# A two-layer diffusion trunk: norm and next modulation joined, half of the norm's subtractions on GpSimd, the output written by channel halves

## The reference, cut to what matters

```python
def modulate(x, shift, scale):
    return x * (1 + scale) + shift

def trunk_layer(x, mod, p, ctx):
    shift, scale, gate = mod[:, :, :, 0], mod[:, :, :, 1], mod[:, :, :, 2]
    h = modulate(x, shift[:, :, 0], scale[:, :, 0])
    x = layer_norm(ALPHA * x + 0.5 * gate[:, :, 0] * swiglu(h, p['ffn_w_gu'][0], p['ffn_w_down'][0]),
                   p['ln_g'][0], p['ln_b'][0])
    h = modulate(x, shift[:, :, 1], scale[:, :, 1])
    u, state = token_mixing(h, p, ctx)
    x = layer_norm(ALPHA * x + gate[:, :, 1] * u, p['ln_g'][1], p['ln_b'][1])
    h = modulate(x, shift[:, :, 2], scale[:, :, 2])
    x = layer_norm(ALPHA * x + 0.5 * gate[:, :, 2] * swiglu(h, p['ffn_w_gu'][1], p['ffn_w_down'][1]),
                   p['ln_g'][2], p['ln_b'][2])
    return x, state
```

## Time and profile before

| | |
|---|---|
| median of 3 runs | 3199.32 us (3198.49 to 3204.26) |
| the profiled execution | 3201.78 us, of which the span of its records is 3200.0 us |
| PE busy | 2974.8 us, 93% of the span |
| DVE, ACT, POOL busy | 1289.7, 914.8 and 144.8 us |
| PE in the chain that ended last | 84% of the span |

### The profile page before, as it was taken

How to read it: one execution, slowest core, us unless ns; L and a number is a source line. 1 busy time by engine, 2 the same in 40 slices (tenths; PEclk the granted TensorE clock), 3 DMA queues, 4 the chain that set the end, 5 groups by cost and what they waited for, 6 DMA issues and landing times.

```text
span 3200.0 us, 46489 instructions
## 1 busy us (share of the span) xinstructions
PE 2974.8 (93%) x20109; PEld 2613.6 (82%) x20109; DVE 1289.7 (40%) x1789; ACT 914.8 (29%) x1270; POOL 144.8 (5%) x88
## 2 busy tenths in 40 slices
PE   6999998998789899999979999989987998999997
PEld 5999997776546599999979999967755455999996
DVE  3233235445545442322542322364363546233226
ACT  3221223322245132222252212233223434221222
POOL 0000000104200000000000000001050000000000
PEclk8999999999889999999989999999997999999998
DMA  8223233103220122322532232421142101223221
GB/s 297 66 66 87 79 107 116 53 27 118 93 86 7 47 66 66 85 78 72 162 105 72 65 91 70 134 72 53 53 143 96 33 1 53 79 59 93 72 62 52
DMA packets 359017, 259.03 MB, mean 81 GB/s; under 512 B 27152, under 2 KB 310100, under 8 KB 358740
## 3 DMA queue, kind: packets, MB, share of 16 engines
q1 hardware_dynamic: 358868, 256.85, 26.6%
HBM read 253.25 MB, written 3.57 MB: 80 GB/s over the span
## 4 chain that ended last, share of the span: by engine, by line
PE 84%; DVE 8%; ACT 3%; DMA 2%; issue 1%; SPq 1%; POOL 0%; DVEq 0%; ACTq 0%; PEldq 0%; POOLq 0%
PE banks L729 54%; PE banks L645 15%; PE banks L596 2%; ACT arena L1250 2%; PE banks L1164 1%; PE banks L844 1%; PE banks L1187 1%; DVE x_res L1808 1%; PE banks L1015 1%; PE banks L1201 1%; DMA w_slots<-in_w_mod 1%; PE banks L1157 1%; DMA w_slots<-in_ffn_w_down 1%; DVE w_split L1687 1%; PE banks L910 1%
## 5 line engine op out<-in xcount | busy, mean ns | idle before, releaser
L729 PE MATMUL banks<-h_hi,w_split 128*128 128x320 f32 x5376 | 1184.5, 309 | 1.1 <-DVE mod L1636 1.1
L729 PEld LDWEIGHTS banks<-h_hi,w_split 128*128 128x128 f32 x5376 | 899.4, 188 | 1.5 <-issue 1.5
L729 PE MATMUL banks<-h_lo,w_split 128*128 128x320 f32 x2688 | 830.6, 309 | 0.0
L729 PE MATMUL banks<-hid_hi,w_split 128*128 128x320 f32 x2816 | 624.5, 310 | 0.1
L1687 DVE TENSOR_TENSOR w_split<-w_slots,w_split 128x2048 fp32r<-128x2048 f32 x152 | 348.3, 2292 | 422.1 <-ACT w_split L1250 422.0
L729 PEld LDWEIGHTS banks<-h_lo,w_split 128*128 128x128 f32 x2688 | 504.5, 188 | 0.0
L1250 ACT ACTIVATE arena<-banks 128x640 f32<-128x640 f32 (+8 forms) x336 | 170.1, 537 | 1137.9 <-PE banks L729 804.4
L729 PEld LDWEIGHTS banks<-hid_hi,w_split 128*128 128x128 f32 x2816 | 472.2, 188 | 2.0 <-issue 1.6
L729 PE MATMUL banks<-hid_lo,w_split 128*128 128x320 f32 x1408 | 435.3, 309 | 0.0
L1250 ACT ACTIVATE w_split<-w_slots 128x2048 fp32r<-128x2048 f32 x152 | 290.1, 1909 | 405.6 <-PE banks L729 371.2
L1751 DVE TENSOR_TENSOR arena<-arena,banks 128x640 f32<-128x640 f32 x88 | 72.2, 821 | 767.1 <-ACT arena L1250 767.1
(11 more groups left out here) (258 smaller groups left out, 2563.0 us busy)
## 6 DMA issues: line engine op xcount, KB each, us to landing
w_slots<-in_ffn_w_gu SPq DMA_DIRECT2D x176, 512.0 KB, 5.1
w_slots<-in_ffn_w_down SPq DMA_DIRECT2D x64, 384.0 KB, 3.7
w_slots<-in_w_mod SPq DMA_DIRECT2D x12, 2048.0 KB, 7.9
arena<-in_w_mod SPq DMA_DIRECT2D x10, 2048.0 KB, 12.9
w_slots<-in_ffn_w_down SPq DMA_DIRECT2D x64, 320.0 KB, 4.3
h_mod<-in_w_mod SPq DMA_DIRECT2D x8, 2048.0 KB, 7.9
mixed<-in_w_mod SPq DMA_DIRECT2D x6, 2048.0 KB, 8.9
w_slots<-in_w_in SPq DMA_DIRECT2D x6, 2048.0 KB, 8.0
```

The lines of the kernel that those rows point to most:

```text
L729: ins = mm(banks[:, b0 + hf, 0:HALF], w[:, k, :], x[:, k, t], start=w is wlo and k == 0, stop=w is whi and x is hi and k == kt - 1, skip_g ...
```

## The change

Gain and bias of a norm are no longer applied to `X` where a modulation follows. VectorE forms, from the modulation's scale and shift and the norm's gain and bias, a joint factor and addend (`compose`, three instructions of 128 x 8 for each half of the channels, into `JOINT`), and ScalarE's `modulate` applies these to the normed tile straight away (`normed` in place of `affine`). The residual gets gain and bias with ALPHA in `scale_residual`, 8 instructions for one, from vectors scaled at the start (`LNS`). Only the last norm of layer 1 still has its own gain and bias on ScalarE.

GpSimd subtracts `DELTA` from tiles 4 to 7 (`shift(sub)` in its list, four instructions a norm), VectorE keeps tiles 0 to 3 and waits for `shifted` ahead of tiles 4 to 7. Modulation pieces 12 and 14 (first halves of shift and scale) change places with 13 and 15: the former are now computed in the token mixers, the latter in norm 1. In `ffn(0)`, `parameters()` stands ahead of `settle(0, 4)`. SyncE fills the third modulation of a swiglu after down job 6's weights, not after job 5's. Low parts of the input tiles are made within norm 2 as in norm 1. At the end transposes, copies and stores go through half 0 of all token tiles first, then half 1, with 10 stores of 256 KB.

Left out of the diff: semaphore names and counts, the allocation of `LNS` and `JOINT`, and places where 12 and 14 are only renamed.

```diff
--- before.py
+++ after.py
...
@@ -147,7 +147,7 @@
-FIRST_MODS, RING_MODS = (0, 2, 1, 3, 4, 5), (10, 11, 13, 15, 16, 17)
+FIRST_MODS, RING_MODS = (0, 2, 1, 3, 4, 5), (10, 11, 12, 14, 16, 17)
@@ -160,7 +160,7 @@
     if sub < 2:
-        return [((l, 8), (l, 9)), ((l, 12), (l, 14))][sub]
+        return [((l, 8), (l, 9)), ((l, 13), (l, 15))][sub]
     return [(l + 1, 2), (l + 1, 3)] if l + 1 < DEPTH else []
...
@@ -268,7 +270,7 @@
                     MOD_AT[x] = (hmod, mixed)[n][:, 0:SLOT]
-            MOD_AT[l, 12], MOD_AT[l, 14] = hmod[:, 0:SLOT], arena[:, 0:SLOT]
+            MOD_AT[l, 13], MOD_AT[l, 15] = hmod[:, 0:SLOT], arena[:, 0:SLOT]
             for i in RING_MODS:
...
@@ -510,7 +512,7 @@
                                     fill_mod(*mods[1])
-                                elif m == 5:
+                                elif m == 6:
                                     sp.wait_ge(mod_row, mod_at[mods[0]] + 1)
...
@@ -571,11 +573,13 @@
-            for t in range(NCH):
-                sp.wait_ge(fin_copy, 2 * t + 2)
-                dst = a["y_s"][0, t * P:(t + 1) * P, :] if t < 4 else a["y_p"][0]
-                sp.dma_start(dst, XIN[:, t, :]).then_inc(fin_store, 16)
-            sp.wait_ge(fin_store, 16 * NCH)
+            for n in range(2 * NCH):
+                half, t = n // NCH, n % NCH
+                cols = slice(half * 512, (half + 1) * 512)
+                sp.wait_ge(fin_copy, n + 1)
+                dst = a["y_s"][0, t * P:(t + 1) * P, cols] if t < 4 else a["y_p"][0, :, cols]
+                sp.dma_start(dst, XIN[:, t, cols]).then_inc(fin_store, 16)
+            sp.wait_ge(fin_store, 32 * NCH)
...
@@ -1219,9 +1223,9 @@
-            pe.wait_ge(s["affine"], DEPTH * 24)
             for n in range(2 * NCH):
-                t, half = n // 2, n % 2
+                half, t = n // NCH, n % NCH
+                pe.wait_ge(s["affine"], 4 * half + 4)
                 if n >= 4:
@@ -1294,21 +1298,24 @@
-                    MOD = MODS[l]
+                    plain = l == 0 and sub == 0
+                    shift, scale = (MODS[l][:, sub, i] if plain else JOINT[:, i] for i in range(2))
                     for m in range(KT_M):
-                        if m % 4 == 0:
-                            act.wait_ge(mod_done, max(mod_at[l, 6 * sub + m // 4], mod_at[l, 6 * sub + 2 + m // 4]) + 1)
+                        if m % 4 == 0 and plain:
+                            act.wait_ge(mod_done, max(mod_at[l, m // 4], mod_at[l, 2 + m // 4]) + 1)
+                        elif m % 4 == 0:
+                            act.wait_ge(s["composed"], o["composed"] + 2 * (sub - 1) + m // 4 + 1)
                         if m == 0 and (l or sub):
-                            act.wait_ge(mod_row, mod_at[l, (3, 9, 14)[sub]] + 1)
+                            act.wait_ge(mod_row, mod_at[l, (3, 9, 15)[sub]] + 1)
                         if l or sub:
-                            act.wait_ge(s["affine"], o["affine"] + 8 * (sub - 1) + m + 1)
+                            act.wait_ge(s["normed"], o["normed"] + 8 * (sub - 1) + m + 1)
                         at = 8 * (sub // 2) + m
...
                             ins = f(dst[:, t0:t0 + n], X[:, m, t0:t0 + n], ACT.Identity,
-                                    scale=MOD[:, sub, 1, m, g:g + 1], bias=MOD[:, sub, 0, m, g:g + 1])
+                                    scale=scale[:, m, g:g + 1], bias=shift[:, m, g:g + 1])
                         ins.then_inc(s["modded"], 1)
@@ -1612,8 +1619,8 @@
                 layer_norm(2, (lambda: weights_hi(2 * FFN_JOBS + 1)) if l + 1 < DEPTH else None)
-                for m in range(KT_M):
-                    act.wait_ge(s["normed"], o["normed"] + m + 1)
+                for m in range(KT_M if l + 1 == DEPTH else 0):
+                    act.wait_ge(s["normed"], o["normed"] + 16 + m + 1)
                     f(X[:, m, :], X[:, m, :], ACT.Identity, scale=PTS1[l][:, R_LNG + 16 + m:R_LNG + 17 + m],
@@ -1647,6 +1654,7 @@
                     link(ins)
+                link(v.tensor_scalar(LNS[l][:], PTS1[l][:, R_LNG:R_LNG + 48], float(ALPHA), None, ALU.mult))
             dve.sem_inc(par1_ready, 1)
@@ -1686,13 +1694,31 @@
-                def input_lo_tile(sub, m):
-                    dve.wait_ge(s["h_hi"], o["h_hi"] + 8 * (sub // 2) + m + 1)
+                def input_lo_tile(n, m):
+
+                    dve.wait_ge(s["h_hi"], o["h_hi"] + 8 * n + m + 1)
                     v.tensor_tensor(HLO[:, m], GATE[:, m % 2], HHI[:, m].bitcast(F32), ALU.subtract).then_inc(s["h_lo"], 1)
...
                     dve.wait_ge(s["modded"], o["modded"] + 8 * (sub + 1))
-                    link(v.tensor_scalar(X, X, float(ALPHA), None, ALU.mult))
+                    if l == 0 and sub == 0:
+                        link(v.tensor_scalar(X, X, float(ALPHA), None, ALU.mult))
+                        return
+                    ln, at = (LNS[l], 8 * (sub - 1)) if sub else (LNS[l - 1], 16)
+                    for m in range(KT_M):
+                        ins = v.tensor_scalar(X[:, m, :], X[:, m, :], ln[:, at + m:at + m + 1], ln[:, 24 + at + m:25 + at + m], ALU.mult, ALU.add)
+                    link(ins)
+
+                def compose(sub, half):
+
+                    ln, sn = (l, sub + 1) if sub < 2 else (l + 1, 0)
+                    ms = slice(4 * half, 4 * half + 4)
+                    shift, scale = MODS[ln][:, sn, 0, ms], MODS[ln][:, sn, 1, ms]
+                    dve.wait_ge(mod_done, max(mod_at[ln, 6 * sn + half], mod_at[ln, 6 * sn + 2 + half]) + 1)
+                    gain, bias = (bc(PTS1[l][:, r + 8 * sub + 4 * half:r + 8 * sub + 4 * half + 4].unsqueeze(2), [P, 4, 2]) for r in (R_LNG, R_LNB))
+                    link(v.tensor_tensor(JOINT[:, 0, ms], scale, bias, ALU.mult))
+                    v.tensor_tensor(JOINT[:, 1, ms], scale, gain, ALU.mult)
+                    finish(v.tensor_tensor(JOINT[:, 0, ms], JOINT[:, 0, ms], shift, ALU.add), "composed", 2 * sub + half + 1)
@@ -1789,12 +1815,12 @@
                                 dve.wait_ge(f_freed[n % 2], o["f_freed"][n % 2] + n // 2 + 1)
+                                if sub == 0 and m == 4:
+                                    parameters()
                                 settle(sub, m)
...
                                     mod_add(*mods[m // 5], 3)
-                                if sub == 0 and m == 4:
-                                    parameters()
@@ -1816,39 +1842,32 @@
                         mod_add(*mods[0], 3)
+                        compose(sub, 0)
                     if meanwhile:
...
                     shift(1)
-                    if not meanwhile:
-                        shift(2)
                     dve.wait_ge(s["rstd"], o["rstd"] + sub + 1)
                     for m in range(KT_M):
-                        if m == 4 and meanwhile:
-                            shift(2)
-                        if m == 6:
-                            shift(3)
                         if m == 1 and mods:
                             mod_add(*mods[1], 3)
-                        if sub == 2:
-                            v.tensor_tensor(X[:, m, :], X[:, m, :], RS[:], ALU.mult).then_inc(s["normed"], 1)
-                            continue
-                        link(v.tensor_tensor(X[:, m, :], X[:, m, :], RS[:], ALU.mult))
-                        v.tensor_scalar(X[:, m, :], X[:, m, :], PTS1[l][:, R_LNG + 8 * sub + m:R_LNG + 8 * sub + m + 1],
-                                        PTS1[l][:, R_LNB + 8 * sub + m:R_LNB + 8 * sub + m + 1], ALU.mult, ALU.add).then_inc(s["affine"], 1)
-                        if sub == 1:
-                            if m >= 2:
-                                input_lo_tile(2, m - 2)
+                            compose(sub, 1)
+                        if m >= 4:
+                            dve.wait_ge(s["shifted"], o["shifted"] + 4 * sub + m - 3)
+                        v.tensor_tensor(X[:, m, :], X[:, m, :], RS[:], ALU.mult).then_inc(s["normed"], 1)
+                        if m >= 2 and sub and mods:
+                            input_lo_tile(sub, m - 2)
                     if sub == 1:
                         weights_lo(FFN_JOBS + 1)
-                        input_lo_tile(2, 6)
-                        input_lo_tile(2, 7)
+                    if sub and mods:
+                        input_lo_tile(sub, 6)
+                        input_lo_tile(sub, 7)
...
                     weights_lo(0)
-                for m in range(KT_M):
-                    input_lo_tile(0, m)
-                    if l == 0 and m == 3:
-                        weights_lo(1)
+                    for m in range(KT_M):
+                        input_lo_tile(0, m)
+                        if m == 3:
+                            weights_lo(1)
                 scale_residual(0)
@@ -2140,6 +2159,12 @@
                 o = offsets[l]
+                def shift(sub):
+                    pool.wait_ge(s["delta_copied"], o["delta_copied"] + sub + 1)
```

(20 more changed lines are left out.)

## The result

The changed kernel takes 3182.06 us (median of 4 runs, 3177.82 to 3186.89), the kernel before on the same chip 3198.90. The ratio is 0.9946, 95% interval 0.9930 to 0.9962: 17 us faster (12 to 22). The forecast was 3179.2 us, in a range of 3161 to 3188.

The account below looks back on a forecast made before the run. TensorE holds 84% of the chain, so only its idle time and the tail can be won. Parameters -17.4, norm 0 +3.8, norm 1 +0.6, norm 2 -5.0, end -2.1: -20.1 us, giving 3179.2 us (range 3161 to 3188).

Parts of the forecast that it names:

- Parameters first: Swiglu 0, both layers: TensorE's 12.9 us wait for `par` goes, with slow matmuls and products behind it; -17.4 us.
- The price of a shift: Norms and end: GpSimd's shifts alternate with VectorE's two-input instructions, one whole instruction at a time, 1.2 us per shift.
- norm 0: Norm before the first projection, twice: ScalarE's first modulation starts later, +1.9 us each; -0.65 each without contention.
- The end: Last norm to the final stores: copies end earlier despite two GpSimd shifts among the multiplications, -2.1 us; -4.1 without contention.
- No contention: Rival, chance 0.20: GpSimd's shifts do not hold VectorE up; -37.1 us in sum, 3162.2 us.
- norm 1: Norm before the second swiglu, twice: last low parts and k-tiles end later, +0.3 us each; -3.0 each without contention.
- norm 2: Norm from layer 0 into layer 1: first modulation takes the first affine's place, -5.0 us; -8.3 without contention.
- GpSimd as a wait of its own: Rival, chance 0.06: each GpSimd shift is 2.5 us of work in norms and end; +28.6 us, 3207.8 us.
- `par` as a wait that moves: Rival, chance 0.06: TensorE's wait in swiglu 0 only moves to job 7's bank or weights; 17.4 us back, 3196.6 us.

Follow-up runs that it names:

- e2_vector: The changed kernel with the shifts of tiles 4 to 7 back on VectorE at their former places; 3163.31 us, ratio 0.9886 to the kernel before.
- e3_late: The changed kernel, but GpSimd waits for the first multiplication by rstd before its shifts, in all norms but the last; 3176.47 us, ratio 0.9925 to before.
- e4_half: The changed kernel with each GpSimd shift cut into two instructions of 320 columns; 3179.66 us, ratio 0.9934 to the kernel before.
- e5_own: e2_vector plus GpSimd copies, two-input subtractions or fills on data no other engine touches, one kind in each of three norms; 3168.55 us, one run.

## Why the prediction was right

*Parameters first*: -17.03 measured, -17.4 forecast. The wait went and nothing took its place, with or without SyncE's fill moved. The one step that was off is the product behind the matmuls: I took it down to 9.69, the time of the last down job, and it takes 9.88 (0.35 us less than before in layer 0 and 0.25 in layer 1, instead of 0.54 in each).

*The price of a shift* carried the rest: 1.2 us a turn, taken from ends in the mixers. The runs show it to be right in kind (GpSimd's whole instructions in turn with VectorE's, down to an 8-column `compose`, whoever's data it is) and near in size: +2.41 for norm 0 against +1.9, +0.7 against +0.3, -4.64 against -5.0. Each norm lost some 0.4 us more than forecast; with the 1.28 of one alone four turns make 0.3 of it. GpSimd did not slip in after each `compose`: of the three in norm 0 the first lost 0.2 us, the second a whole turn, the third nothing. That the shifts would all lie ahead of the first multiplication was nearly so there: the fourth turn holds that multiplication itself up.

*The end*: -1.95 against -2.1. The eight multiplications take 8.71 us, 2.7 more than eight of 0.75: two of GpSimd's turns fall among them, as forecast, at 1.35 and not 1.0 each. e2_vector gains 3.1 there (4.28 - 1.15), short of the 4.1 without contention: VectorE's own shift among the multiplications costs it 1.5.

*The rivals.* "No contention" is not how the kernel ran, but its sum is near to e2_vector, where VectorE does the shifts alone: -34.7 by the stages, against -37.1; norm 1 -3.1 (-3.0), norm 2 -8.24 (-8.3). Where VectorE has a shift on the path there is less: at the end, and in norm 0, -0.02 for -0.65; with that shift moved it is -0.65 there too. GpSimd as a wait of its own, and `par` as a wait that moves, did not come.

What the prediction did not say, though its sums held it: with 17.4 us from one part, the other three were worth 2.7 (measured 0.3). Nor did it weigh that a shift left on VectorE (0.75 us a tile, half of 1.49) is cheaper than a turn (some 1.25), so that the offload was a loss.

What stays open is why the mixers differ by up to 6 us between traces, and the start by 3. In the mixers TensorE waits for the modulations' weights as long in both traces (13.6 and 14.0 us in layer 1), so it is not the loads. Where they came out shorter the mean granted clock was higher (0.90 for 0.86 at the start; 0.93 for 0.92 in layer 1's mixers, with TensorE busy for 5.4 us less), but the longest mixers, 485.70 us in e3_late, had 0.93 too: the clock can be a part of it, not all.

## What to carry to other kernels

Before two-input work is moved from VectorE to GpSimd, look at what VectorE has queued at that time: if it reads two tensors from SBUF, each GpSimd instruction that reads SBUF can be a wait of up to that instruction's length, also for an operand of 8 columns, and may cost more than the work that it takes away. If several parts are changed at once, cut both traces at the same points of the chain and add up the stages: that shows in one trace which part pays and which takes back. A short wait of TensorE also costs what its clock loses: here 12.9 us of waiting for a copy were worth 17.0, 3.5 of the rest in the slow matmuls and 0.6 in the products behind them.

## What the hardware showed

- Two halves cost GpSimd more than one whole: in e4_half the second to fourth begin 0.81 us apart (535.33, 536.14, 536.96) for 320 columns, against 1.28 for 640. The kernel gained all the same, since VectorE waits for one piece at a time.
- GpSimd's fill of 128 x 640 took 0.63 us beside VectorE's shifts and held nothing up; its copy of that size, with one input, did: alone it took 0.71 us (at 533.85 in e5_own; the 1.03 above is a mean in which the first copy waits for shift 0).
